# Split-precision input products: the high and low activations side by side, in one 512-column product

## The reference

```python
h = rms_norm(x, norm_mix[l])
proj = h @ w_in[l]
(dq, dk, dv, dz, da, db, mq, mk, mv, lx, ly, gates) = split_columns(proj)
y_dn = gated_deltanet(dq, dk, dv, dz, da, db, ...) @ dn_out[l]
y_mb = moba_attention(mq, mk, mv) @ mb_out[l]
y_lru = rg_lru_branch(lx, ly, ...) @ lru_out[l]
g = jax.nn.sigmoid(gates + b_gate[l]).reshape(b, t, 3, d)
x = x + (g[:, :, 0] * y_dn + g[:, :, 1] * y_mb + g[:, :, 2] * y_lru) @ w_o[l]
gate, up = jnp.split(rms_norm(x, norm_ffn[l]) @ ffn_in[l], 2, axis=-1)
x = x + (jax.nn.silu(gate) * up) @ ffn_down[l]
```

## Time and profile before

| | us |
|---|---|
| median of 3 runs | 910.72 |
| the profiled execution | 911.29 |
| its span, first to last instruction | 909.5 |
| PE busy | 898.0 |
| DVE busy | 661.5 |
| ACT busy | 513.9 |

### The profile page before, as it was taken

The page is one execution under the profiler, slowest core; times in us unless marked ns, Lnnn a source line. Parts: engine busy times, 40 slices in busy tenths (PEclk is TensorE's granted clock), DMA queues, the critical chain, the costliest instruction groups (busy, mean ns, idle before and its releaser), DMA issues.

```text
span 909.5 us, 13892 instructions
## 1 busy us (share of the span) xinstructions
PE 898.0 (99%) x5460; PEld 765.8 (84%) x5460; DVE 661.5 (73%) x1096; ACT 513.9 (56%) x877; POOL 2.4 (0%) x6
## 2 busy tenths in 40 slices
PE   8999999999999999999999999999999999999996
PEld 5999899788887888888879998988888888888885
DVE  6879876797968665656688797767978675665756
ACT  7586555875446444445465766568644554444443
POOL 0000000000000000000000000000000000000000
PEclk9999999999999999999999999999999999999999
DMA  8544435456664777677755344255656567767761
GB/s 308 196 157 163 146 112 162 162 197 231 206 224 158 214 200 255 201 220 250 216 179 171 117 163 138 96 181 190 229 192 205 184 215 216 252 196 231 237 202 47
DMA packets 99281, 173.22 MB, mean 190 GB/s; under 512 B 53136, under 2 KB 59024, under 8 KB 99216
## 3 DMA queue, kind: packets, MB, share of 16 engines
q1 hardware_dynamic: 98928, 172.26, 58.6%
q10 hardware_dynamic: 288, 0.08, 0.0%
HBM read 165.49 MB, written 6.82 MB: 189 GB/s over the span
## 4 chain that ended last, share of the span: by engine, by line
PE 93%; DVE 4%; ACT 1%; DMA 1%; issue 0%; SPq 0%; DVEq 0%; ACTq 0%
PE bank L542 7%; PE bank L444 7%; PE bank L445 7%; PE bank L446 7%; PE bank L543 7%; PE bank L544 7%; PE bank L347 5%; PE bank L348 5%; PE bank L349 5%; PE bank L619 5%; PE bank L386 5%; PE bank L387 5%; PE bank L388 5%; PE bank L375 2%; PE bank L376 2%; PE bank L374 2%
## 5 line engine op out<-in xcount | busy, mean ns | idle before, releaser
L877 ACT CAST whi<-raw 128x1024 fp32r<-128x1024 f32 x292 | 305.8, 1053 | 301.5 <-PE bank L446 94.9
L1217 DVE TENSOR_TENSOR wlo<-raw,whi 128x1024 fp32r<-128x1024 f32 x292 | 350.2, 1216 | 74.6 <-ACT whi L877 72.0
L347 PE MATMUL bank<-ahi,whi 128*128 128x256 f32 x448 | 129.6, 289 | 0.8 <-DVE tmp L1267 0.8
L348 PE MATMUL bank<-alo,whi 128*128 128x256 f32 x448 | 126.6, 283 | 0.0
L349 PE MATMUL bank<-ahi,wlo 128*128 128x256 f32 x448 | 126.6, 283 | 0.0
L542 PE MATMUL bank<-whi,ahi 128*128 128x512 f32 x288 | 114.4, 397 | 1.4 <-DVE small L1299 0.8
L544 PE MATMUL bank<-whi,alo 128*128 128x512 f32 x288 | 112.3, 390 | 0.0
L444 PE MATMUL bank<-whi,ahi 128*128 128x512 f32 x288 | 112.2, 390 | 0.0
L543 PE MATMUL bank<-wlo,ahi 128*128 128x512 f32 x288 | 112.2, 390 | 0.0
L446 PE MATMUL bank<-whi,alo 128*128 128x512 f32 x288 | 112.1, 389 | 0.0
L445 PE MATMUL bank<-wlo,ahi 128*128 128x512 f32 x288 | 112.0, 389 | 0.0
(11 more groups left out here) (270 smaller groups left out, 1301.2 us busy)
## 6 DMA issues: line engine op xcount, KB each, us to landing
raw<-stream_dram SPq DMA_DIRECT2D x292, 512.0 KB, 4.6
turned_dram<-proj SPq DMA_DIRECT2D x144, 32.0 KB, 1.7
proj<-turned_dram SPq DMA_DIRECT2D x18, 256.0 KB, 4.6
proj<-gbias_dram SPq DMA_DIRECT2D x12, 256.0 KB, 4.6
par<-params_dram SPq DMA_DIRECT2D x2, 556.5 KB, 7.5
x<-x_dram SPq DMA_DIRECT2D x2, 512.0 KB, 5.3
mixture_dram<-proj SPq DMA_DIRECT2D x16, 64.0 KB, 1.9
proj<-mixture_dram SPq DMA_DIRECT2D x2, 512.0 KB, 3.9
```

The source lines that it names most:

```text
L347: pe.matmul(dst, whi_of(m)[:, wcol], hi, start=first, stop=False, skip_group_check=True)
L348: pe.matmul(dst, whi_of(m)[:, wcol], lo, start=False, stop=False, skip_group_check=True)
L877: act.copy(whi_of(m), raw_of(m)).then_inc(*AC.up(("hi", m), "w"))
L1217: dv.tensor_tensor(wlo_of(m), raw_of(m), whi_of(m), ALU.subtract).then_inc(*DV.up(("lo", m), "w"))
```

## The change

`ahi` and `alo` become two halves of one array, `parts[:, kt, 0 or 1, :]`, side by side for each k tile. The weights of the fourteen chunks are laid out by output tile: a step now holds all eight k tiles of one output tile `n`, which is complete after one step, in bank `n` (0 or 1). For ten chunks (`SUMMED`: the six of `CONVS`, 12, 13, 14, 15) the high weights multiply both parts in one product of 512 columns, whose right half (high by low) stays a separate sum; low by high is added to the left half. When the tile is done, ACT copies the right half to `proj`, and DVE adds the left half from PSUM to it (`sum`). For the chunks 6 to 9 (`COPIED`) the three products of 256 columns stay, and ACT copies each tile. A tile's bank must be empty again two steps after it was begun (`emptied`). The convolution and its first tap (L957, L1267) read `proj` and no longer the bank. The ACT copies of chunks 6 to 9 move from `side` to `taps`, ahead of `hi`. The order of the chunks and of the other work stays.

```diff
+SUMMED = CONVS + LX + (14, 15)
+COPIED = (6, 7, 8, 9)
-        ahi = sb("ahi", [P, KT, T], F32R)
-        alo = sb("alo", [P, KT, T], F32R)
+        parts = sb("parts", [P, KT, 2, T], F32R)
+        ahi, alo = parts[:, :, 0, :], parts[:, :, 1, :]
...
+        def emptied(c, n):
+            return (DV, ("sum", c, n)) if c in SUMMED else (AC, ("in", c, n))
+
+        def finished(chunks, k):
+
+            return [(c, n) for c in chunks for n in range(2) if AT[c] + 1 + n == k]
...
-            def by_output(l, k, dst, start_kt):
-
-                for i in range(4):
-                    kt = start_kt + i
-                    for n in range(2):
-                        ins = products(dst[:, n * T:(n + 1) * T], cols(2 * i + n), l * NH + k,
-                                       ahi[:, kt, :], alo[:, kt, :], kt == 0 and n == 0, kt == KT - 1)
+            def by_output(l, k, c, n):
+
+                m, main = l * NH + k, bank[n][:, 0:T]
+                for kt in range(KT):
+                    if c in SUMMED:
+                        pe.matmul(bank[n][:, :], whi_of(m)[:, cols(kt)], flat(parts[:, kt, :, :]), start=kt == 0, stop=kt == KT - 1, skip_group_check=True)
+                        ins = pe.matmul(main, wlo_of(m)[:, cols(kt)], ahi[:, kt, :], start=False, stop=kt == KT - 1, skip_group_check=True)
+                    else:
+                        ins = products(main, cols(kt), m, ahi[:, kt, :], alo[:, kt, :], kt == 0, kt == KT - 1)
                 ins.then_inc(*PE.up(("bulk", k)))
...
-                            pe.wait_ge(*(AC.at(l, ("in", 15)) if t else DV.at(l, ("xc", 1))))
+                            pe.wait_ge(*DV.at(l, ("sum", 15, t)))
...
-                        if n > 1 and half == 0:
-                            by, name = in_copied(FM[n - 2])
+                        if n:
+                            by, name = emptied(FM[n - 1], half)
                             pe.wait_ge(*by.at(l, name))
-                        by_output(l, k, bank[n % 2], 4 * half)
+                        by_output(l, k, FM[n], half)
...
             def taps(l, k):
 
+                for c, n in finished(COPIED, k):
+                    rows = slice(32 * (2 * (c % 2) + n), 32 * (2 * (c % 2) + n) + 32)
+                    act.wait_ge(*PE.at(l, ("bulk", k - 1)))
+                    act.copy(proj[:, in_tile(c, n), :], bank[n][:, 0:T]).then_inc(*AC.up())
+                    act.copy(proj[rows, ROT + 2 * (c // 8), :], bank[n][rows, 0:T]).then_inc(*AC.up(("in", c, n)))
+                for c, n in finished(SUMMED, k):
+                    act.wait_ge(*PE.at(l, ("bulk", k - 1)))
+                    if c in CONVS[2:]:
+                        act.wait_ge(*DV.at(l, ("conv", CONVS.index(c) - 2)))
+                    act.copy(proj[:, in_tile(c, n), :], bank[n][:, T:2 * T]).then_inc(*AC.up(("small", c, n)))
                 if k in CONV_AT:
                     c = CONV_AT.index(k)
-                    act.wait_ge(*PE.at(l, ("bulk", k - 1)))
...
                     for i in range(2):
-                        act.activation(tmp[:, c % 2, i * T:(i + 1) * T], in_bank(CONVS[c])[:, i * T:(i + 1) * T], ACT.Copy,
+                        act.wait_ge(*DV.at(l, ("sum", CONVS[c], i)))
+                        act.activation(tmp[:, c % 2, i * T:(i + 1) * T], proj[:, in_tile(CONVS[c], i), :], ACT.Copy,
...
...
             def side(l, k):
+                for c, n in finished(SUMMED, k):
+                    dv.wait_ge(*AC.at(l, ("small", c, n)))
+                    step(dv.tensor_tensor(proj[:, in_tile(c, n), :], bank[n][:, 0:T], proj[:, in_tile(c, n), :], ALU.add), ("sum", c, n))
```

More of the change, by code:

```diff
@@ L254, in gu_bank, with in_tile @@
             return bank[(2 * j - 2 + t) % 3 if j else 4 + t]
[L256 to L265, removed]
+        def in_tile(c, n):
+            return 56 + 2 * (CONVS.index(c) % 2) + n if c in CONVS else 2 * c + n
+        def emptied(c, n):
+            return (DV, ("sum", c, n)) if c in SUMMED else (AC, ("in", c, n))
+        def finished(chunks, k):
+            return [(c, n) for c in chunks for n in range(2) if AT[c] + 1 + n == k]
         def by_transfer(j):
@@ L965, in taps @@
                         t = 2 * (c - 12) + i
-                        act.activation(proj[:, XC + t, :], in_bank(c)[:, i * T:(i + 1) * T], ACT.Identity, bias=p_("convb", t),
+                        act.wait_ge(*DV.at(l, ("sum", c, i)))
+                        act.activation(proj[:, XC + t, :], proj[:, in_tile(c, i), :], ACT.Identity, bias=p_("convb", t),
                                        scale=p_("conv", TAPS * (12 + t) + 3)).then_inc(*AC.up(("xtap", c - 12)))
@@ L1028, in side @@
                         act.activation(Vb[:, g, :], b3(2 + g // 4, 4)[:, g % 4, :], ACT.Copy, scale=sm["vsc"][:, g:g + 1]).then_inc(*AC.up("vb"))
[L1029 to L1036, removed]
                 if k == MV0 + 4:
@@ L1131, in side @@
                         q = 2 * hf + i
-                        act.activation(flat(ahi[:, 2 * q:2 * q + 2, :]), mix_turned(hf, i), ACT.Copy, scale=0.5).then_inc(*AC.up(("mixhi", q)))
+                        act.activation(ahi[:, 2 * q:2 * q + 2, :], mix_turned(hf, i).rearrange("p (k t) -> p k t", k=2), ACT.Copy, scale=0.5).then_inc(*AC.up(("mixhi", q)))
                 if k == 2 * FFN0:
@@ L1434, in side @@
                     dv.wait_ge(*AC.at(l, ("tap", c)))
-                    conv(l, [in_bank(CONVS[c])[:, i * T:(i + 1) * T] for i in range(2)], [tmp[:, c % 2, i * T:(i + 1) * T] for i in range(2)],
+                    conv(l, [proj[:, in_tile(CONVS[c], i), :] for i in range(2)], [tmp[:, c % 2, i * T:(i + 1) * T] for i in range(2)],
                          [OFF["conv"] + TAPS * (2 * CONVS[c] + i) for i in range(2)], ("conv", c))
@@ L1539, in side @@
                     r = ROT + 2 * (k == 23)
-                    dv.wait_ge(*AC.at(l, ("rows", 7 if k == 13 else 9)))
+                    dv.wait_ge(*AC.at(l, ("in", 7 if k == 13 else 9, 1)))
                     step(dv.stream_shuffle(proj[:, r + 1, :], proj[:, r, :], [(i + 16) % 32 for i in range(32)]), ("shuffle", k == 23))
@@ L1549, in side @@
                     dv.wait_ge(*DV.at(l, ("cossin", k == 29)))
-                    dv.wait_ge(*AC.at(l, ("in", 7 if k == 15 else 9)))
+                    dv.wait_ge(*AC.at(l, ("in", 7 if k == 15 else 9, 1)))
                     for h in range(HEADS):
@@ L1590, in side @@
                     dv.wait_ge(*AC.at(l, ("xtap", c - 12)))
-                    conv(l, [in_bank(c)[:, i * T:(i + 1) * T] for i in range(2)], [proj[:, XC + 2 * (c - 12) + i, :] for i in range(2)],
+                    conv(l, [proj[:, in_tile(c, i), :] for i in range(2)], [proj[:, XC + 2 * (c - 12) + i, :] for i in range(2)],
                          [OFF["conv"] + TAPS * (2 * c - 12 + i) for i in range(2)], ("xc", c - 12))
@@ L1658, in side @@
                         dv.wait_ge(*AC.at(l, ("mixhi", q)))
-                        step(dv.scalar_tensor_tensor(out=flat(alo[:, 2 * q:2 * q + 2, :]), in0=mix_turned(hf, i), scalar=0.5,
-                                                     in1=flat(ahi[:, 2 * q:2 * q + 2, :]).bitcast(F32), op0=ALU.mult, op1=ALU.subtract),
+                        step(dv.scalar_tensor_tensor(out=alo[:, 2 * q:2 * q + 2, :], in0=mix_turned(hf, i).rearrange("p (k t) -> p k t", k=2), scalar=0.5,
+                                                     in1=ahi[:, 2 * q:2 * q + 2, :].bitcast(F32), op0=ALU.mult, op1=ALU.subtract),
                              ("mixed", q))
@@ L1799 @@
     stream = np.zeros((L * CH, P, 2 * HALF), np.float32)
-    wi = _columns(turned).reshape(L, KT, P, C_IN, 256).transpose(0, 3, 2, 1, 4).reshape(L, C_IN, P, 2 * HALF)
+    wi = _columns(turned).reshape(L, KT, P, C_IN, 2, P).transpose(0, 3, 2, 4, 1, 5).reshape(L, C_IN, P, 2 * HALF)
     z, mv = (win[:, :, a:a + 512].reshape(L, 2, 4, P, 512).transpose(0, 1, 3, 2, 4).reshape(L, 2, P, 2 * HALF) for a in (1536, 3080))
```

## The result

| | before | after |
|---|---|---|
| median | 910.75 us (4 runs, 910.6 to 913.13) | 927.7 us (4 runs, 925.68 to 928.78) |
| ratio | | 1.0177, 95% interval 1.0165 to 1.0189 |
| profiled span | 909.5 us | 926.8 us |
| granted clock over the span | 0.998 | 0.994 |

A forecast was written before the change was run, and what follows sets the result against it. PE was taken to bound the kernel (busy 898.0 of 909.5 us). Waits of 8.3 us a layer, less 2.0 and 0.4, made 5.9, 11.8 over two layers: from 910.7 to 922.5 us, range 913 to 928.

The forecast's parts named there:

- 347 expected: PE, each k tile: a 512 and a 256 product take 227 + 120 = 347 ns, against 360 before.
- the sum: Forecast total: 8.3 us of waits a layer, less 2.0 and 0.4, is 5.9 slower; two layers 11.8.
- the six places: PE waits a layer: step 10 0.5, step 19 3.2, step 25 0.4, step 26 1.4, step 36 1.5 and 1.3 us.
- the old wait 0.42: PE's wait for a convolution before old step 20, forecast to go: 0.4 us a layer.
- Waits per layer ... = 8.3 us, less 20 x 0.10 = 2.0 and 0.4: Six PE waits a layer, less 0.10 us gained in each of 20 steps and an old convolution wait: 5.9 slower.
- DMA has only more time: Rest of the layer: moves as one with PE, weights arriving for a slower step; no cost put there.
- (a): Rival: the sums hide everywhere and PE gets its gain, 910.7 - 4.8 = 905.9 us; chance 0.13.
- (b): Rival: step 19 alone waits, the rest is in time, 912.3 us, no measurable change; chance 0.09.
- (c): Rival: the pair costs as by the page's gap, PE gain 0.8 and not 4.0 us, 925.7 us; chance 0.06.
- (d): Rival: product durations are the cost, 320 x 180 ns = 57.6 us less, 853 us; chance 0.01.
- (e): Rival: the pair at 320 ns, 8.8 us more gain, half lost in the same waits, 918 us; chance 0.05.

The follow-up runs named there:

- all five: Changed kernel with sums (3, 0), (1, 1), (5, 1), (15, 0) and (15, 1) moved up on DVE: 916.85 us, ratio 1.0056.
- Keeping PE busy: Changed kernel plus 24 unread products of 256 columns on PE at the end of step 18 in each layer: 924.9 us, ratio 1.0147.
- the wait alone: Kernel before, with only a PE wait added before step 19 for DVE's convolution of chunk 1: 922.13 us, ratio 1.0122.
- the two with the SiLU cleared and wide products: Five sums moved plus chunk 1's SiLU ahead of DVE's splits: 915.34 us; the same plus ACT's inverse copies put first: 914.91 us.
- six places cleared: Changed kernel with five sums and chunk 1's SiLU moved up on DVE, ACT's inverse copies put first: 914.91 us, ratio 1.0033.

## Why the prediction was right, point by point

**What a product costs.** Spacing and not duration was the right price: 346 to 353 ns a pair for 347 expected. But the gain was sized too large. From the start of one step to the start of the next, the steps with a pair gain 0.01 to 0.11 us, 0.07 in the mean, where the sum had 0.10. That is 1.35 us a layer for 2.0. The rival by durations (853 us) is out: six undisturbed steps gave 0.47 us, where it has 48 k tiles of 180 ns, or 8.6. The gap that the Trainium skill gives for an isolated product, page "TensorE: Matmul & The Clock Gate", section "Back-to-back issue gap", makes an estimate of 0.12 us for them (2.5 ns saved in each), and the trace does not agree.

**The queue on DVE.** Shown at each of the six places by the trace, and by moving calls alone: the two sums of step 36 gave 4.8 us, all five 10.9. As delays from start to start, which is what the forecast worked out, 8.0 us a layer were measured for 8.3.

**The missed term.** The sum ended at 11.8 us and 17 were measured. Counted from the start of each layer's input chunks, PE's steps end up 7.7 us later in layer 0 and 7.95 in layer 1, where the sum had 5.9. In layer 0 that is: delays 8.0; the clock 1.46; less the old wait 0.42 and the gain of 1.35 for 20 steps. That adds to 7.7. So the step that fell short is "Waits per layer ... = 8.3 us, less 20 x 0.10 = 2.0 and 0.4": it took a standstill to cost its length, and it costs the half clock behind it too. Keeping PE busy took 2.8 us off, and the wait alone in the kernel before cost 11.1 us where the standstill by itself would be 7.4. The second mis-sized term is the gain, 1.3 us too large over both layers. The sum also put nothing for the end of layer 0, with the sentence that "DMA has only more time"; there PE lost 1.3 us (below).

**How near the number was, and why.** The waits were right in place, cause and size, and the direction follows from them. That 927.7 lies inside 913 to 928 is partly luck: its upper end stood for waits a third larger than forecast, and they were not larger. The room was filled by the clock, which the range did not have. Two of the four runs (928.62 and 928.78) lie above 928.

**Parts that rest on one execution.** The span's first product starts 0.75 us later in the profile after (12.98 against 12.23), and so in some of the other traces (0.74 later with five sums moved), but 0.2 earlier in the two with the SiLU cleared and wide products; it is in the difference of the spans and not in the cause. At the end of layer 0 PE waits for `hid` (L1701, 1.1 us; 0 in the kernel before), because ACT gets the last transposed hidden group late from the DMA. ACT's wait for that transfer is 1.68 us in the kernel before, 1.72 in the one with a wait added to it, 3.00 in the changed kernel, and 1.93 to 4.01 in its variants. From the last gate product of layer 0 to the first of layer 1, PE loses 1.3 us against the kernel before in the changed kernel, 0.05 in the one with a wait added, and 0.3 to 2.3 in the variants. Whether the change lengthens the transfer or the executions differ was not tried and stays open; it is 0 to 1.3 us of the result.

**The rivals.** (a), hidden sums (905.9): no. (b), step 19 alone (912.3): no, five of six waits lie elsewhere. (c), the pair saving 2.5 ns and not 13 (925.7): its number is nearer to 927.7 than the forecast's, but by chance. It needs a gain of 0.8 us and no fallen clock, and the steps show a gain of 2.7 us and the clock. (d), durations (853): no. (e), the pair at 320 ns (918): no, 346 to 353 ns. The forecast had 0.66.

That the work as a whole, and not the order, costs: in part. The order of the calls is worth 10.9 of 17 us. With six places cleared, 3.4 us (0.33%) are left over the kernel before, and each further place that was cleared showed another behind it. Two things are in what is left. In the profiled execution of that kernel (span 913.3, 3.8 over the kernel before) 1.0 us is lost in the chunks and gates of layer 0 and 1.2 in those of layer 1, and 2.3 at the end of layer 0, at the transfer. The first part fits the 20 sums and their copies, which take DVE and ACT time on a loop (PE, DVE, ACT and back for the inverse) with little to spare: in the kernel before, ACT's copy in step 26 ends at 105.29 and PE takes it at 105.58, and level 3 ends at 100.58 and PE takes it at 102.01. That this loop and not something else is the reason was not tested. No version was found that beats the kernel before.

## What to carry to other kernels

Price a moving operand by start to start and not by duration: here 512 columns replace two of 256 at 10 ns less, not 180. When a PSUM tile must be emptied within one step in place of two, go through the in-order queue of the emptying engine place by place; the average share of that engine (73%) tells nothing. A standstill of PE of 2.7 us and more was followed by the half clock each time here, which cost some 1.5 us and more, so such a standstill is to be priced with it. Clearing one wait on a tight loop was worth only the slack that the next place had.

## What the runs showed of the hardware that was not expected

In all profiled executions together PE stood still ahead of step 19 eight times for 2.69 to 3.92 us, and each time the granted clock was at half for 3.4 us (six times) or 6.8 us (twice) around the restart or behind it. The length of the wait does not tell which: 3.90 us had 6.8 and 3.92 had 3.4, 2.69 had 3.4 and 2.85 had 6.8. Of the waits of 1.5 to 1.9 us in step 20, two (1.67 and 1.85) were followed by 3.4 us of half clock and four (1.54, 1.57, 1.57 and 1.68) by none, and behind shorter waits (up to 1.49 us) it never fell. So in this middle length the same kernel can go either way.
